# A row maximum subtracted inside the score contraction instead of by its own matmul, in two causal attentions

## The reference

```
# latent attention (first): 12 heads, q and k of 64 + 32 (rotated) dims, v of 64
q_rope = concat(x1*cos - x2*sin, x2*cos + x1*sin)     # rotary halves
s = q @ k.T * 96**-0.5 ; causal mask ; softmax ; @ v
# forget-gate attention (second): 12 heads, q, k, v of 64
s = q @ k.T * 64**-0.5 + F[t] - F[s]                  # F: cumulated log forget gates
    causal mask ; softmax ; @ v
```

## Time and profile before

| | us |
|---|---|
| median of 3 runs | 3333.41 (3331.48 to 3334.3) |
| the profiled execution's own time | 3337.3 |
| its span (first to last instruction) | 3335.5 |
| PE busy | 3072.7 (92%) |
| DVE busy | 1788.6 (54%) |
| ACT busy | 1180.1 (35%) |
| POOL busy | 1051.9 (32%) |

### The profile page before, as it was taken

How to read it: one execution, slowest core, us unless ns; L and a number is a source line. 1 busy time by engine, 2 the same in 40 slices (tenths; PEclk the granted TensorE clock), 3 DMA queues, 4 the chain that set the end, 5 groups by cost and what they waited for, 6 DMA issues and landing times.

```text
span 3335.5 us, 36680 instructions
## 1 busy us (share of the span) xinstructions
PE 3072.7 (92%) x14504; PEld 2536.2 (76%) x14504; DVE 1788.6 (54%) x1799; ACT 1180.1 (35%) x1873; POOL 1051.9 (32%) x418
## 2 busy tenths in 40 slices
PE   5888889999989999999999899999988889998997
PEld 4666668888778888888777787788877777777786
DVE  4888943111352443444478645677744676666533
ACT  3666730000232111001143324577743344545511
POOL 3111024444424444444425133211123212111252
PEclk9999999999989999999999999999999999999998
DMA  2000021111201111111211312200021200000131
GB/s 99 20 26 32 20 88 51 45 51 51 89 26 51 51 51 45 51 51 45 63 39 44 127 49 69 82 20 20 20 82 38 76 32 27 31 26 26 70 114 63
DMA packets 42571, 171.64 MB, mean 51 GB/s; under 512 B 4464, under 2 KB 5488, under 8 KB 41392
## 3 DMA queue, kind: packets, MB, share of 16 engines
q1 hardware_dynamic: 32976, 119.89, 11.4%
q10 hardware_dynamic: 9440, 49.55, 3.8%
HBM read 143.73 MB, written 25.69 MB: 51 GB/s over the span
## 4 chain that ended last, share of the span: by engine, by line
PE 73%; issue 11%; DVE 11%; ACT 3%; POOL 1%; DMA 1%; SPq 0%; ACTq 0%; DVEq 0%; POOLq 0%
PE ps L486 45%; PE ps L1100 4%; PE ps L870 3%; PE aux L999 3%; PE ps L934 3%; PE ps L983 2%; PE ps L658 2%; PE ob L1018 1%; PE ob L1021 1%; PE ob L1019 1%; DVE eb L1960 1%; PE aux L1001 1%; PE ps L678 1%; PE aux L687 1%; DVE zb L1938 1%
## 5 line engine op out<-in xcount | busy, mean ns | idle before, releaser
L434 POOL TENSOR_TENSOR wh<-raw,con 128x1024 fp32r<-128x1024 f32 x203 | 491.4, 2421 | 2223.0 <-PE ps L486 1036.8
L436 POOL TENSOR_TENSOR wl<-raw,wh 128x1024 fp32r<-128x1024 f32 x203 | 552.4, 2721 | 15.9
L486 PE MATMUL ps<-hh,wh 128*128 128x512 f32 x1392 | 437.2, 396 | 23.7 <-POOL wl L436 14.5
L486 PE MATMUL ps<-hl,wh 128*128 128x512 f32 x1392 | 434.8, 394 | 0.0
L486 PE MATMUL ps<-hh,wl 128*128 128x512 f32 x1392 | 434.3, 394 | 0.0
L486 PEld LDWEIGHTS ps<-hh,wh 128*128 128x128 f32 x1392 | 264.6, 191 | 81.6 <-POOL wl L436 16.2
L486 PEld LDWEIGHTS ps<-hl,wh 128*128 128x128 f32 x1392 | 265.4, 191 | 56.2
L486 PEld LDWEIGHTS ps<-hh,wl 128*128 128x128 f32 x1392 | 265.1, 190 | 56.1
L1811 DVE TENSOR_TENSOR px_l<-px,px_h 128x512 fp32r<-128x512 f32 (+3 forms) x288 | 212.9, 741 | 96.8 <-ACT px_h L1641 94.7
L2057 DVE TENSOR_TENSOR y_t<-y_t,ps 128x1024 f32<-128x1024 f32 x120 | 146.5, 1221 | 175.8 <-PE ps L486 175.8
L1344 ACT ACTIVATE ff<-fr 128x1024 f32<-128x1024 f32 x32 | 33.9, 1061 | 558.7 <-DVE fr L2046 558.7
(11 more groups left out here) (414 smaller groups left out, 6463.2 us busy)
## 6 DMA issues: line engine op xcount, KB each, us to landing
raw<-wall SPq DMA_DIRECT2D x211, 512.0 KB, 3.5
spill_x<-x_t ACTq DMA_DIRECT2D x2, 4096.0 KB, 11.1
xold_t<-spill_x ACTq DMA_DIRECT2D x2, 4096.0 KB, 12.5
x_t<-xt SPq DMA_DIRECT2D x8, 512.0 KB, 9.5
spill_o<-op ACTq DMA_DIRECT2D x4, 1024.0 KB, 3.9
o_all<-spill_o ACTq DMA_DIRECT2D x2, 2048.0 KB, 11.0
x_t<-xt ACTq DMA_DIRECT2D x1, 4096.0 KB, 12.9
spill_out<-ot ACTq DMA_DIRECT2D x8, 512.0 KB, 2.6
```

Source lines behind the costliest of these rows:

```text
L434: pool.tensor_tensor(wh[:, s, :, :], raw[:, s, :, :], ones.unsqueeze(1).broadcast_to([P, KT, P]), ALU.mult).then_inc(w_high, 1)
L436: pool.tensor_tensor(wl[:, s, :, :], raw[:, s, :, :], wh[:, s, :, :].bitcast(F32), ALU.subtract).then_inc(w_split, 1)
L486: m = pe.matmul(ps[:, w, a:b], lw[:, sl, k, :], r[:, i, a:b], start=(i == 0 and j == 0), stop=(i == len(ks) - 1 and j == 2))
```

## The change

The row of negated maxima becomes one more row of the contraction. When the four diagonals of a query half are there, PE makes one matmul of `first_r` (32 columns of weights, the first all ones, the others zero) with them: a 32 x 512 result in PSUM, whose first row is the row of negated maxima. ACT copies it to 32 rows of the q operand that the contraction has free, where k has ones. In the latent attention the rows become free because DVE now adds the two rotated halves (rows 64 to 95 and 96 to 127 of `qf`) into one; in the other the bias rows are laid out anew (6 heads in 32 rows, by constants and by the weights of the forget gates). The matmul of ones in each tile is gone. The two blocks 0 and 1 now both stand at step -5 (step 7 of the head before), and each later block one step earlier.

```
+    MAX_AHEAD = {-5: (0, 1), -4: (2,), -3: (3,), -2: (4,), -1: (5,), 0: (6,), 1: (7,)}
+    ROW_AHEAD = {-2: 0, 2: 1}
...
@@ PE, softmax, scores(u)
                 if kb == 0:
-                    pe.wait_ge(dg_ready, M + 8 * h + 4 * c + 4)
+                    pe.wait_ge(mrow_ready, G + 2 * h + c + 1)
...
-                m = pe.matmul(st, ones_r[:, :], dgs[:, c, n0:HALF], start=False, stop=(kb < 4 * c), skip_group_check=True)
...
+            def maxima_row(h, c):
+                pe.wait_ge(dg_ready, M + 8 * h + 4 * c + 4)
+                if c == 0 and h > 0:
+                    pe.wait_ge(ot_made, G + 2 * h - 1)
+                dst = ob[0:32, 0, :] if c == 0 else ps[0:32, mx, HALF:S]
+                pe.matmul(dst, first_r[:, :], dgs[:, c, :], start=True, stop=True, skip_group_check=True).then_inc(mrow_done, 1)
...
@@ PE, the latent loop (the other one is changed alike; maxima_row comes last in a step)
             if 0 <= h < MLA_HEADS:
                 scores(step)
+            for block_of in maxima_of(step, MLA_HEADS):
+                maximum(*block_of)
...
             if step >= AV_LAG:
                 values(step - AV_LAG)
+            rh, rc = row_of(step, MLA_HEADS)
+            if rh is not None:
+                maxima_row(rh, rc)
...
@@ ACT, softmax
+            def maxima_row(h, c):
+                act.wait_ge(mrow_done, G + 2 * h + c + 1)
+                src = ob[0:32, 0, :] if c == 0 else ps[0:32, mx, HALF:S]
+                copy(row_dst(h)[:, c * HALF:(c + 1) * HALF], src).then_inc(mrow_ready, 1)
...
                 if 0 <= step < heads * N_HT:
                     high_part(step)
+                rh, rc = row_of(step, heads)
+                if rh is not None:
+                    maxima_row(rh, rc)
+                for block_of in maxima_of(step, heads):
+                    diagonal(*block_of)
                 if last_of_chunk(done, heads):
                     inverse_sum(done)
...
@@ ACT, before the latent attention
-        copy(ka_h[64:96, :], qf[64:96, :])
-        copy(ka_h[96:P, :], qf[64:96, :]).then_inc(high_ready, 1)
+        copy(ka_h[64:96, :], qf[64:96, :]).then_inc(high_ready, 1)
...
@@ DVE
+        dve.memset(ka_h[96:P, :].bitcast(F32), 1.0)
...
         def latent_rope(h):
             dve.wait_ge(q_done, h + 1)
-            dve.tensor_tensor(qf[HI, :], ps[HI, LATENT, :], trig[HI, :], ALU.mult).then_inc(rope_ready, 1)
+            chain(dve.tensor_tensor(qf[HI, :], ps[HI, LATENT, :], trig[HI, :], ALU.mult))
+            dve.tensor_tensor(qf[64:96, :], qf[64:96, :], qf[96:P, :], ALU.add).then_inc(rope_ready, 1)
...
```

More of the change, by code:

```diff
@@ L359, in program, with of_head, maxima_of, row_of @@
     FETCH_STEP = MLA_LAST - N_HT + 6
-    def maximum_of(step, lead, heads):
-        h, i = divmod(step + lead, N_HT)
-        return (h, i) if i < 8 and h < heads else (None, None)
+    MAX_AHEAD = {-5: (0, 1), -4: (2,), -3: (3,), -2: (4,), -1: (5,), 0: (6,), 1: (7,)}
+    ROW_AHEAD = {-2: 0, 2: 1}
+    def of_head(step, table, heads, nothing):
+        for h in (max(step, 0) // N_HT, step // N_HT + 1):
+            if h < heads and step - h * N_HT in table:
+                return h, table[step - h * N_HT]
+        return None, nothing
+    def maxima_of(step, heads):
+        h, blocks = of_head(step, MAX_AHEAD, heads, ())
+        return [(h, i) for i in blocks]
+    def row_of(step, heads):
+        return of_head(step, ROW_AHEAD, heads, 0)
     def last_of_chunk(u, heads):
@@ L1022, in values @@
                           skip_group_check=True).then_inc(at_done, 1)
-            return maximum, scores, values
+            return maximum, maxima_row, scores, values
         def latent_max_ready(h):
@@ L1032, in latent_parts_ready @@
             pe.wait_ge(kl_ready, h + 1)
-        maximum, scores, values = softmax(
-            MLA_HEADS, MLA_MAX, lambda h: (qa[h % 2][0], ka[h % 2][0]), latent_max_ready,
-            lambda h: [(ka[h % 2][a], qa[h % 2][b]) for a, b in ((0, 0), (0, 1), (1, 0))], latent_parts_ready,
+        maximum, maxima_row, scores, values = softmax(
+            MLA_HEADS, MLA_MAX, lambda h: (qa[h % 2][0][0:96, :], ka[h % 2][0][0:96, :]), latent_max_ready,
+            lambda h: [(ka[h % 2][a][0:rows, :], qa[h % 2][b][0:rows, :]) for a, b, rows in ((0, 0, P), (0, 1, 96), (1, 0, 96))],
+            latent_parts_ready,
             lambda h, kb: (v1[h % 2][:, kb, :], vl[h % 2][:, kb, :]), lambda h: pe.wait_ge(vl_ready, h + 1), dg)
@@ L1064, in _ @@
         evacuated(w7)
-        for step in range(-MLA_LEAD, 0):
-            maximum(*maximum_of(step, MLA_LEAD, MLA_HEADS))
-        for step in range(MLA_HEADS * N_HT + AV_LAG):
+        for step in range(-LEAD, MLA_HEADS * N_HT + AV_LAG):
             h, i = divmod(step, N_HT)
-            if h < MLA_HEADS:
+            if 0 <= h < MLA_HEADS:
                 scores(step)
[L1071 to L1074, removed]
+            for block_of in maxima_of(step, MLA_HEADS):
+                maximum(*block_of)
+            if 0 <= h and h + 1 < MLA_HEADS:
                 if i < 3:
@@ L1662, in tile @@
                     high_part(step)
-                mh, mi = maximum_of(step, lead, heads) if step >= -lead else (None, None)
-                if mh is not None:
-                    diagonal(mh, mi)
+                rh, rc = row_of(step, heads)
+                if rh is not None:
+                    maxima_row(rh, rc)
+                for block_of in maxima_of(step, heads):
+                    diagonal(*block_of)
                 if last_of_chunk(done, heads):
@@ L1694, in y_high @@
             copy(y_h[:, m, :], gate_t[:, m, :]).then_inc(high_ready, 1)
-        for step in range(-MLA_LEAD, MLA_HEADS * N_HT + AV_LAG + 5):
+        for step in range(-LEAD, MLA_HEADS * N_HT + AV_LAG + 5):
             h, i = divmod(step, N_HT)
@@ L2333, in tile @@
             def tile(step):
-                mh, mi = maximum_of(step, lead, heads) if step >= -lead else (None, None)
-                if mh is not None:
-                    maximum(mh, mi)
+                for block_of in maxima_of(step, heads):
+                    maximum(*block_of)
                 if 0 <= step < heads * N_HT:
@@ L2380, in ot_read @@
                 dve.wait_ge(g_made, pair)
-        tile, weighted = softmax(MLA_HEADS, MLA_LEAD, MLA_MAX, inv, ot_read)
-        for step in range(-MLA_LEAD, MLA_HEADS * N_HT + AV_LAG + 2):
+        tile, weighted = softmax(MLA_HEADS, MLA_MAX, inv, ot_read)
+        for step in range(-LEAD, MLA_HEADS * N_HT + AV_LAG + 2):
             h, i = divmod(step, N_HT)
@@ L2386, in _ @@
             if step == 0:
[L2387 removed]
+                dve.tensor_copy(ka2_l[64:96, :], ka_l[64:96, :].bitcast(F32))
             if step == 1:
@@ L2569, in weight_stream @@
     slabs += list(tiles_of(w_in_b[:, 2316:2572]))
-    slabs += list(tiles_of(padded(w_in_b, [(16 * q, 2304, 2316) for q in range(8)])))
+    slabs += list(tiles_of(padded(w_in_b, [(8 * q, 2304 + 6 * (q // 4 % 2), 2310 + 6 * (q // 4 % 2)) for q in range(16)])))
     qkv = tiles_of(w_in_b[:, 0:2304])
@@ L2584, in vectors @@
     v[:, V_CONV:V_CONV + 12] = w_conv.reshape(12, P).T
-    for q in range(8):
-        v[16 * q:16 * q + MLA_HEADS, V_BF] = b_f
+    for q in range(16):
+        v[8 * q:8 * q + 6, V_BF] = b_f[6 * (q // 4 % 2):6 * (q // 4 % 2) + 6]
     return v
```

45 lines of the change are left out of this document (23 added, 22 removed).

## The result

The changed kernel is slower: 3398.4 us (3396.8 to 3401.4) against 3333.9 (3331.5 to 3335.0), a ratio of 1.0191 with a 95% interval of 1.0179 to 1.0203, +64.5 us. The forecast was 3374 with a range of 3320 to 3400: the direction and the places were right, the size was too small by 24 us, and the range held by 1.6 us.

A forecast was written before the change was run, and what follows sets the result against it. PE was taken to set the pace (93 to 94% busy). Same-clock terms of +31 us and +10 for the clock gave 3378 on the profiled execution's 3337.3, so 3374 for the median; range 3320 to 3400.

The forecast's parts named there:

- Block 1 behind block 0: PE idles before block 1 for DVE's reduce: +2.35 us a latent head, +3.7 and +1.3 in a pair's heads.
- PE was to come to block 1 0.69 us earlier: Tiles of steps 5, 6 and 7 lose 0.23 us each; DVE's chain gains one of these.
- POOL's stretching of VectorE goes: Second head of a pair: POOL starts behind block 1, so 3.6 us of stretched `px_l` and CAST go.
- Wait before the key-value product: Latent head: PE waits for `qf` behind ACT's copy of the row, about 1 us a head (0.3 to 1.5).
- the add costs nothing beside it: DVE's new add ends at 2215.6, before ACT: no cost; 0.3 us if ACT's copy were away.
- The saving: PE, each head: matmul of ones gone, 2.07 us, two matmuls added, 0.46: -1.61 us, x 24 heads -39 us.
- Sum at the same clock: Latent head +1.7 us (+19 in all), pair +2.4 (+13), first and last heads -1: together +31 us.
- The clock: Lower clock behind 17 new idle times, 0 or up to 2.4 us each: 0 to 41, a fourth taken, +10.
- the working's own highest case: Top of the slower cases: +31 at the same clock and +41 for the clock, +72 us.
- the one that ends faster: PE's saving comes through if DVE reaches the reduce within 0.5 us of block 0's product: 3294 us, chance 0.14.
- The row's round trip: PE to ACT to PE late at step 0 or 4: 0.5 us x 24 = +12, with clock drops 3390, chance 0.09.

The follow-up runs named there:

- e1: Kernel before with only block 1 of the maxima moved directly behind block 0, matmul of ones kept: 3397.5 us, ratio 1.0191.
- e2: Changed kernel with blocks 0 to 3 of the maxima in turn in two halves of their PSUM place: 3328.9 us, ratio 0.9981.
- e4: Kernel before with blocks 0 to 3 of the maxima in turn in two halves of their PSUM place: 3296.1 us, ratio 0.9881.
- e5: Changed kernel with VectorE's low parts of the next head's k (and v) made later, behind the reduces: 3349.9 us, ratio 1.0044.
- e11: Changed kernel without VectorE's add of the two rotated halves of the latent queries: 3394.9 us, ratio 1.0184.
- e7: Changed kernel with two places, later low parts, and PE's row of query half 1 ahead of the projection part: 3301.4 us, ratio 0.9902.
- e12: Changed kernel with two places, blocks 2 and 3 together, row first, without VectorE's add: 3307.8 us, against 3311.6 with the add.
- e6: Changed kernel with two places for blocks 0 to 3 and VectorE's low parts of k (and v) later: 3299.1 us, ratio 0.9896.
- e8: Kernel before with two places for blocks 0 to 3 and VectorE's low parts of k (and v) later: 3296.1 us, ratio 0.9883.
- e3: Changed kernel with 11 unread matmuls of 512 columns between blocks 0 and 1 of each head but the first: 3361.6 us, ratio 1.0082.

## Why the prediction was right, and where it fell short

- *Block 1 behind block 0.* Forecast idle times 3.5, 4.2 and 5.5 us (latent head; first and second head of a pair), measured 3.1 to 3.3 (5.35 in the last head), 3.5 and 4.8. Shown by e1 (the move alone makes the whole loss), e2 and e4 (with a second place it goes) and e5 (shorter queue on VectorE, shorter wait by as much). The step that was a little off: PE was to come to block 1 0.69 us earlier, of which 0.46 were to show as idle time. Against e1, which has no such gain, the idle time is 0.41 us longer in a latent head, but only 0.2 in the first head of a pair and 0 in the second: there small waits of 0.3 to 0.4 for `px_l` and `fkb` have come in ahead of it and take most of the gain.
- *POOL's stretching of VectorE goes.* Right: 2.22 and 2.74 became 0.69 and 0.69, because POOL's start is behind block 1 in PE's order. The rule of the Trainium skill (SBUF — State Buffer, "Who interferes with whom") that these pairs exclude each other fits both traces, and e2's too, where POOL starts early again and `px_l` takes 2.46.
- *Wait before the key-value product.* Forecast 1.0 us, measured 0.5 to 0.7, by the chain that was named (row, copy 0.59, inverse, copy of q). Part of the difference is the row's way to ScalarE: 0.58 us had been counted from the start of its matmul to the copy, 0.35 of it without a row to stand on, and the trace has 0.42 (2157.22 to 2157.64). That the add costs nothing beside it held inside the heads (e11); with the row first it becomes the limit, 0.5 us where 0.3 had been said (e7, e12).
- *The saving.* 1.6 us a head forecast, 1.2 found with most waits gone (e6 against e8). Part of the difference may be that the first matmul behind each wait is 0.1 us longer; that was not tried.
- *Sum at the same clock.* With the measured saving and the measured waits a latent head is -1.2 + 2.1 + 0.6 = +1.5 (forecast 1.7). A pair is -2.4 + 0.6 + 3.1 + 0.7 + 1.2 (the small waits) = +3.2 (forecast 2.4). Together some 34 us where 31 were forecast, against 26 to 34 by e3. That the sum is so near is in part luck: the saving was put 0.4 us a head too high, the small waits at nothing, and the two waits on ScalarE and VectorE too high.
- *The clock*: the mis-sized term. It was counted as a fourth of what it could be at most, +10, because the latent attention ran at 0.99 before and one idle time of 3.25 us had passed without a drop. By e3 it is 37 us in the changed kernel, of which 31 to 38 are new (the estimate of e3), where 10 were forecast. The lower clock came behind all eleven new idle times of the latent attention and behind all of the other attention's, in place of a fourth of them; of the first ten in the latent attention block 1's own matmul shows it in five only (0.58 in three, 0.48 in two, 0.38 in the rest), since in the others the fall began 0.5 to 1.4 us behind its start. Most of the bound (31 to 38 of 41) would have been the right term: the one example at full clock was given too much weight beside the one at 2.51 us and the repeated drops after 4.2 us.

The measured time lies 1.6 us inside the range, whose upper end (3400, +67 on the median before) is below the working's own highest case (+72); that it held is luck.

The rivals: the one that ends faster fell at its own condition (the reduce comes 3 us late, not 0.5). The row's round trip was no bound at step 0 in a latent head; in the other attention it adds 0.44 us in the first head of a pair.

## What to carry to other kernels

When work is regrouped on an in-order engine, look at what used to lie between an instruction and the one that waits for its result elsewhere: that distance was the cover, and the wait's new length can be read from the row of the consumer's queue before anything is built. Give the place written to a second copy before moving such instructions together; here that was worth 39 us without any other change. Count a recurring idle time of PE twice, once for itself and once for the slower matmuls behind it: here the second part was 37 us for 22 of them in the changed kernel.

## What the runs showed of the hardware that was not expected

Matmuls whose result nobody reads, in an idle time that stays as long as it was, made the kernel 37 us faster: the granted clock behind them stayed at its upper level of 2.4 GHz (0.40 us for a matmul in place of 0.63). The length of an idle time alone doesn't tell whether the lower level of 1.2 GHz follows. In the latent attention of the changed kernel it followed all eleven idle times of 3.06 to 5.35 us, though in the kernel before it didn't follow the one of 3.25. In e1 it followed the idle times of 2.64 to 2.76 us in every second head and none of the five of 2.88 between them; in e5 it followed nine of eleven of 1.93 to 2.17 us. What decides it stays open here.
